# Experts' first matrix in whole rows: eight chunks for gate and linear together, four for the second matrix

## What is computed

```python
# 32 experts, each token goes to its best 4; blocks of 128 rows belong to one expert each
def expert_block(args):
    e, toks, wts = args
    u = hf[toks] @ w1[e] + b1[e]                 # w1[e]: 1024 x 2048
    g_, lin = u[:, :D_FF], u[:, D_FF:]           # D_FF = 1024
    g_ = jnp.minimum(g_, SWIGLU_LIMIT)
    lin = jnp.clip(lin, -SWIGLU_LIMIT, SWIGLU_LIMIT)
    y = ((lin + 1.0) * g_ * jax.nn.sigmoid(SWIGLU_ALPHA * g_)) @ w2[e] + b2[e]   # w2[e]: 1024 x 1024
    return y * wts[:, None]
```

## Time and profile before

| | |
|---|---|
| median of 3 runs | 3480.76 us (3476.17 to 3484.16) |
| the profiled execution | 3483.23 us, its span 3481.1 us |
| mean granted clock of PE | 0.979 |
| busy: PE, DVE, ACT, POOL | 3192.4, 2835.2, 1430.8, 735.8 us |
| rounding of expert chunks on ACT | 380 on the page's row, 1916 ns each |
| their rests on DVE | 384, 2284 ns each |
| expert chunks from HBM | 384 of 1 MB, 11.4 us from issue to landing |
| chunks of experts start to flow | at about 450 us, the stage ends at about 1550 us |

### The profile page before, as it was taken

The page is one execution under the profiler, slowest core; times in us unless marked ns, Lnnn a source line. Parts: engine busy times, 40 slices in busy tenths (PEclk is TensorE's granted clock), DMA queues, the critical chain, the costliest instruction groups (busy, mean ns, idle before and its releaser), DMA issues. The chain is left out here.

```text
span 3481.1 us, 38662 instructions
## 1 busy us (share of the span) xinstructions
PE 3192.4 (92%) x13398; PEld 2171.3 (62%) x13398; DVE 2835.2 (81%) x4724; ACT 1430.8 (41%) x1763; POOL 735.8 (21%) x724
## 2 busy tenths in 40 slices
PE   9999989999999999999999999888888888888877
PEld 7877767777777777766787888444344344434432
DVE  7777689999999999967995645888888888888886
ACT  3245357888888888852233632211111111111110
POOL 0001010110110110010000100444444444444443
PEclk8999989999999999999999999999999999999999
DMA  8422279999999999973233025999999999999998
GB/s 287 147 85 104 79 285 398 411 410 405 406 407 404 410 407 402 411 273 120 85 110 126 7 98 215 407 419 421 417 410 410 420 407 413 421 421 405 415 421 347
DMA packets 235414, 1100.56 MB, mean 316 GB/s; under 512 B 21209, under 2 KB 30833, under 8 KB 153073
## 3 DMA queue, kind: packets, MB, share of 16 engines
q0 software_dynamic: 79680, 558.14, 39.2%
q1 hardware_dynamic: 149837, 523.62, 39.2%
q10 hardware_dynamic: 5760, 17.04, 1.2%
HBM read 1069.64 MB, written 33.03 MB: 317 GB/s over the span
## 5 line engine op out<-in xcount | busy, mean ns | idle before, releaser
L2189 DVE TENSOR_TENSOR moe_w_lo<-ring,moe_w_hi 128x2048 fp32r<-128x2048 f32 x384 | 859.5, 2284 | 54.0 <-ACT moe_w_hi L2037 53.1
L2037 ACT ACTIVATE moe_w_hi<-ring 128x2048 fp32r<-128x2048 f32 x380 | 719.3, 1916 | 154.7 <-DMA ring<-in_exp_w 140.0
L2966 PE MATMUL last_banks<-last_rows_b,ring 128*128 128x512 f32 x1024 | 498.4, 633 | 122.9 <-DVE ring L3166 122.6
L2966 PE MATMUL last_banks<-last_rows_a,ring 128*128 128x512 f32 x1024 | 478.6, 611 | 89.0 <-DVE ring L3166 88.9
L3058 ACT ACTIVATE last_gelu<-last_dot 128x2 f32<-128x2 f32 (+1 forms) x257 | 52.3, 203 | 1116.1 <-DVE last_dot L3163 1116.0
L2966 PEld LDWEIGHTS last_banks<-last_rows_b,ring 128*128 128x128 f32 x1024 | 196.4, 201 | 399.3 <-issue 207.3
L2966 PEld LDWEIGHTS last_banks<-last_rows_a,ring 128*128 128x128 f32 x1024 | 188.6, 193 | 334.0 <-issue 198.3
L2845 POOL DMA_INDIRECT last_rows_a<-in_peer_uv,last_ids x256 | 285.9, 1117 | 508.5 <-PE last_banks L2966 330.0
L2845 POOL DMA_INDIRECT last_rows_b<-in_peer_uv,last_ids x256 | 288.8, 1128 | 378.2 <-PE last_banks L2966 357.4
L3166 DVE TENSOR_SCALAR ring<-consts_sb,last_gelu,last_gates 128x128 f32<-128x128 f32 x512 | 161.5, 390 | 75.1 <-ACT last_gelu L3058 74.0
L1785 POOL COPY moe_col<-slots 128x1 uint32 (+1 forms) x30 | 37.0, 1235 | 837.7 <-PE moe_tp L1833 486.2
(11 more groups left out here) (601 smaller groups left out, 6346.7 us busy)
## 6 DMA issues: line engine op xcount, KB each, us to landing
ring<-in_exp_w SPq DMA_DIRECT2D x384, 1024.0 KB, 11.4
ring<-in_w_in SPq DMA_DIRECT2D x38, 1024.0 KB, 5.5
ring<-in_ada_w SPq DMA_DIRECT2D x12, 1024.0 KB, 11.9
z<-in_ada_w SPq DMA_DIRECT2D x12, 1024.0 KB, 5.9
y_rows<-moe_y ACTq DMA_DIRECT2D x17, 512.0 KB, 6.8
ring<-in_w_out SPq DMA_DIRECT2D x8, 1024.0 KB, 5.1
y_rows<-spare SPq DMA_DIRECT2D x1, 7680.0 KB, 26.7
gate_rows<-conv_held ACTq DMA_DIRECT2D x4, 1024.0 KB, 8.1
```

What stands on the lines that cost most here:

```text
L2037: nc.scalar.activation(w_hi[:, slot, :], env.ring[:, slot, :], ACT.Copy).then_inc(hi_done, 1)
L2189: nc.vector.tensor_tensor(w_lo[:, slot, :], env.ring[:, slot, :], w_hi[:, slot, :].bitcast(F32), ALU.subtract).then_inc(lo_done, 1)
L2966: last = nc.tensor.matmul(sums(t)[:, q, :], diag[:, n % SL], slot(n)[:, D + q * W:D + (q + 1) * W], start=first, stop=final)
```

## The change

The first matrix comes in eight chunks of 128 whole rows (2048 columns, "x"), 8 KB in one piece for each partition, then the four of y, in every step. A chunk of x feeds all four banks of gate and linear at once (`first`, `few_first`), with one k a chunk. So gate and linear are full at the same time, after the eighth chunk, and the order of a step is x x x x x x x x y y y y on every engine. The side tasks on PE, ACT and DVE are placed anew; on DVE the clip of the linear part stands apart from the product with the gate. The first expert, the last pair and the overflow path follow the same pattern.

```diff
 def load_chunk(env, sp, e, kind, n, slot, landed):
-    rows = expert_rows(env.d, e, kind, n)
-    if kind == "y":
-        sp.dma_start(env.ring[:, slot, :], rows.rearrange("(p a) n -> p (a n)", a=2)).then_inc(landed[slot], 16)
+    if kind == "x":
+        rows = env.d["exp_w1"][span(e * D + n * P, P), :]
     else:
-        sp.dma_start(env.ring[:, slot, :].rearrange("p (a n) -> p a n", a=2), rows.rearrange("(a p) n -> p a n", p=P)).then_inc(landed[slot], 16)
+        rows = env.d["exp_w2"][span(e * FF + n * 2 * P, 2 * P), :].rearrange("(p a) n -> p (a n)", a=2)
+    sp.dma_start(env.ring[:, slot, :], rows).then_inc(landed[slot], 16)
...
-        order = [("g", n) for n in range(4)] + [("y", n) for n in range(4)] + [("l", n) for n in range(4)]
-        ending = order[0:4] + order[8:12] + order[4:8]
+        order = [("x", n) for n in range(KC)] + [("y", n) for n in range(4)]
...
+            def first(s, slot, k, lhs):
+
+                pe.wait_ge(lo_done, s + 1)
+                for l, w in ((0, w_hi), (0, w_lo), (1, w_hi)):
+                    for q, bank in enumerate(first_banks):
+                        last = nc.tensor.matmul(bank, lhs[l][:, k, :], w[:, slot, q * W:(q + 1) * W], start=k == 0 and l == 0 and w is w_hi, stop=False)
+                last.then_inc(used, 1)
...
+            def biases(b, u):
+                pe.wait_ge(pick_ready, b + 1)
+                bias(glu_ps, u, 0).then_inc(g_done, 1)
+                bias(lin_ps, u, FF).then_inc(l_done, 1)
...
                 pe.wait_ge(glu_done, b)
-                for j in range(4):
-                    few_chunk(at(i, j), slot_of(0, j), j, xt[1][0], glu_ps)
-                    if j == 1:
-                        if not first:
-                            pe.wait_ge(y_parted, n_small)
-                            add_part(y_part, yp).then_inc(y_done, 1)
+                pe.wait_ge(lin_done, b)
+                for j in range(KC):
+                    few_first(at(i, j), slot_of(0, j), j, xt[1][0])
+                    if j == 1 and not at_start:
+                        pe.wait_ge(y_parted, n_small)
+                        add_part(y_part, yp).then_inc(y_done, 1)
+                    if j == 2:
                         turn_hidden(i)
+                    if j == 5:
+                        pe.wait_ge(h_lo, b * 2)
+                        turn_rows(b + 1)
...
+                for j in range(KC):
+                    first(at(i, j), slot_of(1, j), j, xt[0])
+                    if j == 2:
+                        turn_few_hidden(i)
+                    if j == 5 and few_next:
+                        turn_few_rows(b + 1)
+                biases(b, 0)
...
                     round_chunk(slot_of(0, j), (eights + (8 + j) // SL + 1) * 16)
-                    if j == 2 and not first:
+                    if j == 1 and not at_start:
                         rows_part(i - 1, at(i, 0))
                     if j == 4:
                         round_hidden(i)
-                        if not first:
+                        if not at_start:
                             few_rows_out(i - 1, n_small - 1)
-                    if j == 6:
-                        glu_part(b, at(i, 4))
-                    if j == 8:
+                    if j == 7:
                         round_rows(b + 1, 0)
                     if j == 9:
-                        gate_of(b, HALF)
-                rows_out(i, at(i, 8))
+                        glu_part(b, at(i, KC))
+                        lin_part(b, at(i, KC))
+                gate_of(b, HALF)
...
                     round_chunk(slot_of(1, j), (eights + (20 + j) // SL + 1) * 16)
-                    if j == 2:
-                        lin_part(i, at(i, 0))
-                    if j == 7:
+                    if j == 1:
+                        rows_out(i - 1, at(i, 0))
+                    if j == 4:
                         round_few_hidden(i)
+                    if j == 7 and few_next:
+                        round_few_rows(b + 1)
+                    if j == 10:
                         gate_of(b)
-                    if j == 9 and few_next:
-                        round_few_rows(b + 1)
...
                     rest_of_chunk(at(i, j), slot_of(1, j))
-                    if j == 3:
+                    if j == 0:
                         hidden(i, HALF)
-                    if j == 7:
+                    if j == 5:
                         rest_of_few_hidden(i)
-                    if j == 9 and few_next:
+                    if j == 8 and few_next:
                         rest_of_few_rows(b + 1)
-                    if j == 11:
-                        hidden(b)
+                    if j == 10:
+                        clip(b)
```

More of the change, by code:

```diff
@@ L1856, in few_chunk, with second @@
                         for q in range(2):
-                            last = nc.tensor.matmul(bank[:, q, :], both[:, k, :], w[:, slot, a * D + q * W:a * D + (q + 1) * W],
+                            last = nc.tensor.matmul(yp[:, q, :], both[:, k, :], w[:, slot, a * D + q * W:a * D + (q + 1) * W],
                                                     start=k == 0 and w is w_hi, stop=k == KC - 1 and w is w_lo)
+                last.then_inc(used, 1)
+            def second(s, slot, n, lhs):
+                pe.wait_ge(lo_done, s + 1)
+                for a in range(2):
+                    k = 2 * n + a
+                    for l, w in ((0, w_hi), (0, w_lo), (1, w_hi)):
+                        for q in range(2):
+                            last = nc.tensor.matmul(yp[:, q, :], lhs[l][:, k, :], w[:, slot, a * D + q * W:a * D + (q + 1) * W],
+                                                    start=k == 0 and l == 0 and w is w_hi, stop=k == KC - 1 and l == 1)
                 last.then_inc(used, 1)
@@ L1943, in last_step @@
                 pe.wait_ge(glu_done, b)
-                for j in range(4):
-                    chunk(at(i, j), slot_of(0, j), j, xt[1], glu_ps)
+                pe.wait_ge(lin_done, b)
+                for j in range(KC):
+                    first(at(i, j), slot_of(0, j), j, xt[1])
                     if j == 1:
@@ L1948, in last_step @@
                         add_part(y_part, yp).then_inc(y_done, 1)
+                    if j == 2:
                         turn_hidden(i)
-                pe.wait_ge(pick_ready, b + 1)
-                bias(glu_ps, 1, 0).then_inc(g_done, 1)
-                pe.wait_ge(lin_done, b)
-                for j in range(4):
-                    chunk(at(i, 4 + j), slot_of(0, 4 + j), j, xt[1], lin_ps)
-                bias(lin_ps, 1, FF).then_inc(l_done, 1)
+                biases(b, 1)
                 pe.wait_ge(h_lo, b * 2)
@@ L2002, in _ @@
                     pe.wait_ge(pick_ready, b + 1)
-                    for j in range(8):
-                        chunk(o * 12 + MAIN_CHUNKS + j, j, j % 4, xt[0], (glu_ps, lin_ps)[j // 4])
+                    for j in range(KC):
+                        first(o * 12 + MAIN_CHUNKS + j, j, j, xt[0])
                     bias(glu_ps, 0, 0).then_inc(g_done, 1)
@@ L2259, in _ @@
             dve.wait_ge(issued, 1)
-            for j in range(6):
+            for j in range(8):
                 rest_of_chunk(j, j)
-            rest_of_chunk(6, 6)
             rest_of_few_rows(1)
-            rest_of_chunk(7, 7)
             overflow_tables()
-            to_small(0, first=True)
+            clip(0)
+            to_small(0)
             with dve.Fori(0, (N_EXP - 4) // 2) as i2:
```

137 lines of the change are left out of this document (57 added, 80 removed).

## The result

| | before | after |
|---|---|---|
| median of the runs compared | 3482.46 us (3476.17 to 3490.52) | 3592.38 us (3590.01 to 3595.18) |
| ratio, 95% interval | | 1.0316 (1.0291 to 1.0340) |
| span of the profiled execution | 3481.1 us | 3592.2 us |
| one turn of the experts' loop | 65.7 us | 73.2 us |

The account below looks back on a forecast made before the run. Transfers set the pace at 65.7 us a turn; after the change ACT's in-order waits for PE would make it 71.6. 15 x 5.9 = 89 us on 3483.2 gave 3572, 3570 against the median; range 3505 to 3610.

Parts of the forecast that it names:

- The walk: Longest closed way round one turn of the experts' loop through PE, ACT and DVE: 71.6 us, 5.9 over 65.7.
- leg 2: DVE in the experts' loop: seven rests (chunks 8 to 11, 0 to 2) and side steps, 18.7 us.
- leg 5: DVE in the experts' loop: chunk 5, the rest of the hidden rows, chunks 6, 7, 8, 10.1 us.
- leg 6: PE's full stretch, chunk 8 to the next chunk 5, with side work and two short waits for DVE: 32.2 us.
- Legs 3 and 4: PE's half-size chunk 2 and eight transposes, 3.1 us; then ACT's hidden rows, small output and chunk 5, 4.2 us.
- rival D: PE's clock falls in each half stretch, 2 us a turn more: 3600; upper end of the forecast, which together had 0.78.
- How often: Fourteen turns, and the halves ahead of and behind the loop as one: 15 x 5.9 = 89 us.
- A: Transfers still set the pace; 8 KB pieces give 0.8 us a turn, 12 in all: 3469, chance 0.09.
- B: No change: new waits replace landing waits one for one, DMA no faster with larger pieces: 3481, chance 0.05.
- C: Slower by half: legs 3 and 4 run beside DVE, 3 us less a turn, 68.6: 3525, chance 0.08.

Follow-up runs that it names:

- run 1: The changed kernel with side tasks on ACT and PE placed 3 to 4 chunks behind their release, as before, instead of 2: 3468.45 us, 0.9948 of before.
- run 2: The changed kernel with side tasks on ACT 3 chunks behind their release on PE, instead of 2: 3500.74 us.
- run 3: The changed kernel, one corner at a time: next small rows two chunks later on ACT and DVE, 3575.93 us; hidden and next rows one chunk later, 3537.17 us.
- run 5: The kernel before with ACT's tasks moved up to 2 chunks behind release: first 3672.20 us; second, large hidden rows left after rounding 4, 3567.25 us.
- loops of 6: Second-matrix chunks in 4 KB instead of 8 KB pieces: first in the changed kernel with longer leads, 3474.79 us; second in the kernel before, 3483.53 us.

## Why the prediction was right, and where it fell short

**The mechanism** was that of the forecast: ACT's in-order waits for PE in place of its waits for landings. Runs 1, 2, 3 and 5 show it from four sides: longer leads take the loss away, leads in between take part of it, single corners give their own share, and short leads make the old order slow.

**The walk** can be set against one turn of the changed kernel, leg by leg. PE begins to turn the small rows at 922.01 and again at 995.41, 73.4 us later.

| leg | predicted | measured | from, to |
|---|---|---|---|
| 1 PE turns, ACT rounds rows and chunk 8 | 3.3 | 3.2 | 922.01, 925.25 |
| 2 DVE, chunks 8 to 11, 0 to 2 | 18.7 | 18.5 | 925.25, 943.77 |
| 3 PE chunk 2, hidden rows turned | 3.1 | 2.8 | 943.77, 946.58 |
| 4 ACT hidden rows, small output, chunk 5 | 4.2 | 4.7 | 946.58, 951.24 |
| 5 DVE chunk 5 to 8 | 10.1 | 11.7 | 951.24, 962.92 |
| 6 PE's full stretch | 32.2 | 32.5 | 962.92, 995.41 |

The ends that rows show are these (DVE at both ends of leg 2, the second being 939.29 + 4.48, and in leg 5; PE at the ends of leg 6). Legs 3 and 4 meet here where ACT begins with the first half of the hidden rows, at 946.58 above; the prediction had PE done with both halves there, so one leg is shorter and the other longer.

```profile
922.01 0.71 PE L1823 MATMUL moe_tp<-consts_sb,moe_xg 64*128 64x64 f32 x8
```

```profile
925.25 2.29 DVE L2186 TENSOR_TENSOR moe_w_lo<-ring,moe_w_hi 128x2048 fp32r<-128x2048 f32 x1 [1.91 <-ACT moe_w_hi L2035]
...
939.29 4.48 DVE L2186 TENSOR_TENSOR moe_w_lo<-ring,moe_w_hi 128x2048 fp32r<-128x2048 f32 x2
...
951.24 2.29 DVE L2186 TENSOR_TENSOR moe_w_lo<-ring,moe_w_hi 128x2048 fp32r<-128x2048 f32 x1 [3.06 <-ACT moe_w_hi L2035]
953.45 1.28 DVE L2181 TENSOR_TENSOR moe_hidt_lo<-moe_tp,moe_hidt_hi 128x512 fp32r<-128x512 f32 x2
954.64 4.48 DVE L2186 TENSOR_TENSOR moe_w_lo<-ring,moe_w_hi 128x2048 fp32r<-128x2048 f32 x2
960.57 2.29 DVE L2186 TENSOR_TENSOR moe_w_lo<-ring,moe_w_hi 128x2048 fp32r<-128x2048 f32 x1 [1.45 <-ACT moe_w_hi L2035]
```

```profile
962.92 0.73 PE L1876 MATMUL moe_yp<-moe_w_hi,moe_hidt_hi 128*128 128x512 f32 x2 [1.15 <-DVE moe_w_lo L2186]
...
995.41 0.71 PE L1823 MATMUL moe_tp<-consts_sb,moe_xg 64*128 64x64 f32 x8
```

**The term that was mis-sized is leg 5**, 10.1 us predicted and 11.7 measured. DVE has 10.1 us of work there, and on top of it stands 1.45 us for ACT (the row at 960.57), which stands 2.85 for PE's next rows (957.65 above), since PE did chunk 5 at half its clock. In the turn from 753.79, where the clock stayed, DVE does not stand there, and its leg is 806.03 to 816.21, 10.2 us:

```profile
806.03 2.29 DVE L2186 TENSOR_TENSOR moe_w_lo<-ring,moe_w_hi 128x2048 fp32r<-128x2048 f32 x1 [3.05 <-ACT moe_w_hi L2035]
...
809.44 6.77 DVE L2186 TENSOR_TENSOR moe_w_lo<-ring,moe_w_hi 128x2048 fp32r<-128x2048 f32 x3
```

The prediction had this as rival D, at 2 us a turn for which it gave no row, and had the 3 us pause of PE at chunk 5 among the things to look for. It set the two side by side as cases, where the fall came behind that pause in twelve turns of fourteen. The run with the filled pause gives the walk without it, 71.9 us, and so do the two turns, with 71.95 and 71.96, beside the 71.6 of the sum. Thus 3570 fell short by 22 us, 14 times the 1.6 between 71.6 and 73.2. The forecast's walk and D's fall of the clock came true together, inside the range. (PE's idle time, 8 to 9 us a turn in D, is 7.7 by the prediction's own numbers, 71.6 less 63.9, and was 7.1, from 1025.3 less 926.1.)

**How often.** Fifteen times the loss of one turn was put; it was 14 in the loop and 5.0 + 0.9 = 5.9 around it, less than a fifteenth turn of 7.5; no run takes these 5.9 apart.

**What would show it**, point by point: a turn of 70 to 73 us, 73.2; DMA share under 0.97 and some 370 GB/s, 0.95 and 366; ACT's landing waits near nothing, none on record; ACT's waits for PE 10 us a turn or more, 18; DVE's waits for ACT 8 to 10, 10.8 and so a little over; PE's pause at chunk 5 some 3, 2.87.

**The rivals.** A (transfers set the pace, faster) did not come, but its kernel exists: with longer leads the same chunks and order run at 3468, at a turn of 64.4. The prediction put A at 3469 for the pieces alone; they give part of it, so that the two numbers meet is in part luck. The point from which A decides was given as 2 chunks and 5.5 us of distance from ACT to PE; by the runs a task has to stand more than 3 chunks behind its release, since 3 still left 66.6. B and C are out by time, and C also by the row at 951.24: DVE did stand there, for 3.06 us. The remark that DVE must run some 3 chunks further ahead in the new order was not tested by itself; run 1, with that order and the same 8 slots, has no loss that would show a want of room.

**The rules weighed.** Leg 6 rests on 231 ns a matmul, and measured 32.5. By the Trainium skill, "TensorE: Matmul & The Clock Gate", section "Back-to-back issue gap", an estimate of 216 ns would make it 30.3 with everything else as predicted. The page gives that figure as the gap of an isolated matmul, and about 131 ns for a stream of weight loads and matmuls, which is further off; the trace, with 231, decides. The Trainium skill, "DMA: Bandwidth & Descriptors", section "Why small descriptors are slow (HBM only)", counts 3 cycles a packet, from which the prediction estimated 0.5 us a turn for the pieces of sixteen chunks; by the loops of 6 it is 0.3 to 0.8, with which that agrees.

## What to carry to other kernels

When a table of places says after which step an engine takes a side task, write down for each task the distance to the step that releases it, and compare that with how far the engines really stand apart; waits that cost nothing that shows at a distance of four chunks cost 2 us a turn at three and 9 at two here, for the whole queue behind them. A slower layout need not be at fault: here the new chunks and their order are 0.5% faster than the old ones as soon as the tasks are placed at the old distances. And when the walk finds a pause on PE that comes back in every turn, look what the granted clock does behind it, and put its price into the sum instead of keeping it as a separate case.

## What the runs showed of the chip beyond that

PE's granted clock fell to 0.50 behind a pause of 2.9 us in twelve of fourteen turns, and ten matmuls on zeros in the pause kept it at 1.00 and made the kernel 14 us faster. In the loops of runs 1 and 2 and of the version with later hidden rows, where the longest wait of PE's weight loads for DVE was 1.7 to 1.9 us, it was 1.00 (as in the first loop of 6, where the longest reached 2.8). In the three other loops with short leads, the small rows' version of run 3, the second of run 5 and the first of run 5, the longest was 3.4, 3.1 and 4.8 us (the last put down to no engine), and the clock 0.98, 0.98 and 0.93; in the changed kernel it was 3.4 and 0.98. Pieces of 4 KB and 8 KB differ by 0.4 us in eight chunks of 1 MB with the long leads (411 against 414 GB/s), and by less than can be told in the kernel before.
